# Five raw weight buffers and five ring slots, low parts dealt out by stage, and a bias table made on 128 rows

## The chip, the cores and the metric

One core of a Trainium2 chip runs the whole program. The metric is device time in microseconds, from three runs: 1275.13, 1270.58 and 1267.05, median 1270.58. Engines are named as the profile names them: PE is TensorE, ACT ScalarE, DVE VectorE, POOL GpSimd, SP SyncE.

## The reference

A batch of one, 256 tokens, width 1024, everything in float32. Two hybrid layers come first. Each computes, cut to what matters:

```
p  = split(rmsnorm(x, norm_g) @ w_in)          # 9,312 columns of weights
hm = mlstm(silu(conv4(q, k)), v, gates i, f)   # 4 heads of 256, chunkwise with log gates
hg = gla(q, k, v, log_sigmoid(a @ w_a)/16)     # 4 heads, decay per key channel
hd = top-64 sparse attention(q, k, v, index scores) + rel_bias[t5_bucket(distance)]
x  = x + concat(norms and gates of hm, hg, hd) @ w_out
```

A second block follows: a SwiGLU FFN of width 2816 (added with factor 0.5), a mixer, another such FFN and a last rmsnorm. The mixer takes causal attention with 8 heads and a gMLP branch with spatial products over chunks of 128, multiplies each by its own branch weight and by a sigmoid gate, sums them and multiplies by w_out. Every matrix is used once, for 256 tokens, so the program is a stream of weights.

## The kernel before

Activations lie transposed, channels on partitions and tokens along the free dimension. All weights are cut into 364 slots of 128x1024 float32 (512 KB), numbered in the order of use: 90 slots for each layer (74 in, 16 out), 66 for FFN1, 20 + 16 for the mixer's inputs and gates, 8 branch and 8 output slots, and 66 for FFN2.

Each slot passes a pipeline. SP loads it into one of RAW raw buffers. ACT copies it into one of RING ring slots as fp32r, which keeps the high bits (the high part, L392). Then DVE or POOL subtracts the high part from the raw weight, which gives the low part (L854 as one instruction of 1024 columns, L291 as two halves of 512). PE makes three products per tile, high x high, low x high and high x low, 24 matmuls of 256 columns a slot (L1509 with activations as the moving side, L1557 for the output sums, L1547 with 12 matmuls of 512 columns for value slots). RAW is 3 and RING is 6. The helper `split(p)` makes the part of slot g = p + RING after slot p has been used. ACT waits there for `slots_used` and for the load; DVE takes the low part where g is a multiple of 3, POOL takes the others. The last part releases the raw buffer (semaphores `lo`), and SP then loads slot g + RAW into it.

The order on each engine is written out by hand: every engine walks the slot numbers p, runs the jobs of a table `jobs` (or `jobs2` in the mixer) for that p, and then does its share of `split(p)`. The engines' instruction streams are in order, so a wait in a job holds what stands behind it. The layers are a loop of two iterations over one written-out body; the FFNs are loops over four tiles of three slots (gate, up, down).

At a stage's start the first slots (6 in a layer, 8 in the mixer, 4 in an FFN) run on unnormed activations while the norm factor is computed; `early_result` scales their results. ACT's `norm` and DVE's `norm_lo` (L910) then write the normed activations xs. In slots 16 to 25 of a layer eight levels of the gla decay go round DVE (`level_distance` L1067, `level_queries`, `level_take`), ACT (exponentials), POOL (`level_keys` L318) and PE (L1693). In slots 26 to 41 DVE convolves (L1154).

At the program's very start PE multiplies rel_bias by a one-hot matrix into four rows, ACT copies them to SBUF, and ACT's DMA queue stores them to a DRAM table of [4, 128, 384], each row broadcast 128 times (L438). Skewed reads of that table give the bias tiles later. The index scores reuse the SBUF rows, so they wait until the store is done.

In the mixer `spatial` makes the gMLP product on DVE and writes it to y. For the branch slots ACT and DVE then write the high and low parts of y to ys and xs (`branch_hi` L773, `branch_lo` L1418), and PE waits for four low parts before each half of the first branch slot.

Of the kernel before, what the change touches and what calls it, by code (L numbers as in the profile page):

```python
# [21 lines left out]
F32 = mybir.dt.float32  # L22
# [6 lines left out]
P = 128  # L29
D = 1024  # L30
T = 256
# [3 lines left out]
RAW = 3  # L35
RING = 6
# [8 lines left out]
IN_SLOTS, OUT_SLOTS = 74, 16  # L45
LAYER_SLOTS = IN_SLOTS + OUT_SLOTS
# [42 lines left out]

LEVELS = 8  # L90
# [19 lines left out]
EARLY, M_EARLY = 6, 8  # L110
# [22 lines left out]
def build(nc, d, out):  # L133
    ctx = ExitStack()
    with ctx:
# [63 lines left out]
        bias_row = lg[0:4, 0, 0:HOT]  # L199
        pT = gs  # L200

# [38 lines left out]
        def _(sp):  # L240
            sp.dma_start(raw[:, 0, :], d["w"][0]).then_inc(slot_in[0], 16)
            for c in range(N_UPDATES):
                sp.dma_start(x[:, 2 * c:2 * c + 2, :], d["x"][:, 2 * c:2 * c + 2, :]).then_inc(x_in[c], 16)
            for s in range(1, RAW):
                sp.dma_start(raw[:, s, :], d["w"][s]).then_inc(slot_in[s], 16)
            sp.dma_start(const[:, C_LEV:], d["const"][:, C_LEV:]).then_inc(S["rest_in"], 16)
            sp.dma_start(par2[:], d["par2"]).then_inc(S["par2_in"], 16)
            def load(p, slot, reg=0, per=0):

                sp.wait_ge(lo[p % RAW], reg * (per // RAW) + p // RAW)  # L250
                sp.dma_start(raw[:, p % RAW, :], d["w"][reg * per + slot]).then_inc(slot_in[p % RAW], 16)

            def in_order(first, end):
                n = (end - first) // RAW
                if n:
                    with sp.Fori(0, n) as i:
                        for s in range(RAW):
                            load(first + s, first + s, i, RAW)
                for p in range(first + RAW * n, end):
                    load(p, p)  # L260

            def ffn(at):

                with sp.Fori(0, FFN_TILES - 2) as i:
                    for s, turned in enumerate((1, 2, 0)):
                        load(at + 4 + s, at + 4 + turned, i, 3)

            in_order(RAW, FFN1_AT + 4)
            ffn(FFN1_AT)
            in_order(FFN1_AT + FFN_SLOTS - 2, FFN2_AT + 4)  # L270
            ffn(FFN2_AT)
            in_order(TOTAL_SLOTS - 2, TOTAL_SLOTS)
# [10 lines left out]
        def _(pool):  # L283
            def split(p, reg=0, per=0):

                g = p + RING
                if g % RAW:
# [45 lines left out]
            def ffn(at):  # L333
                for p in range(4):
                    split(at + p)
                loops = (FFN_TILES - 2) // 4 - (1 if at == FFN2_AT else 0)
                with pool.Fori(0, loops) as i:
                    for p in range(12):
                        split(at + 4 + p, i, 12)
                for p in range(at + 4 + 12 * loops, at + FFN_SLOTS):  # L340
                    if p + RING < TOTAL_SLOTS:
                        split(p)
# [21 lines left out]
        def _(act):  # L364
            step = Steps(act, S["act_steps"])
            act.dma_start(par[:], d["par"][0]).then_inc(S["par_in"], 16)
            act.dma_start(rb[:], d["rel"]).then_inc(S["rb_in"], 16)
            act.dma_start(hot, d["hot"]).then_inc(S["rb_in"], 16)
            act.dma_start(const[:, 0:C_LEV], d["const"][:, 0:C_LEV]).then_inc(S["const_in"], 16)
# [46 lines left out]
            def norm(n, g, col, used):  # L416
# [16 lines left out]
            act.wait_ge(S["bias_ps"], 1)  # L433
# [3 lines left out]
            act.wait_ge(S["bias_sb"], 1)  # L437
            act.dma_start(bias_rows.ap(), bias_row.rearrange("h (o n) -> h o n", o=1).broadcast_to((4, P, HOT)))\  # L438
                .then_inc(S["bias_out"], 16)
# [3 lines left out]
            with act.Fori(0, LAYERS) as it:  # L443
# [50 lines left out]
                def gate_softplus():  # L494
                    log_and_exp()
# [21 lines left out]
                def forget_softplus():  # L517
                    log_and_exp()
# [160 lines left out]
            def ffn(at, n, h_done, last):  # L679

                def gate_tanh(f, i=0):
                    act.wait_ge(S["ffn_t"], i * 4 + (h_done + f + 1))
# [3 lines left out]
                def product_hi(f, i=0):  # L686
                    act.wait_ge(S["ffn_h"], i * 4 + (h_done + f + 1))
                    act.activation(ys[:, f % YS, 0, :], ca[:, f % 2, :], ACT.Copy).then_inc(S["y_hi"], 1)  # L688

                def next_split(p, i):  # L690
                    if p + RING < TOTAL_SLOTS:
                        split(p, i, 12)

                def four(i, f0):
                    for f in range(f0, f0 + 4):
                        p = at + 4 + 3 * (f - 2)
                        gate_tanh(f, i)
                        next_split(p, i)
                        product_hi(f, i)
                        next_split(p + 1, i)  # L700
                        next_split(p + 2, i)
# [11 lines left out]
                loops = (FFN_TILES - 2) // 4 - (1 if last else 0)  # L713
                with act.Fori(0, loops) as i:
                    four(i, 2)
                if last:
                    four(0, 2 + 4 * loops)
                else:
# [48 lines left out]
            def branch_hi(k):  # L767
# [5 lines left out]
                act.activation(branch(k, 0), y[:, (k + 4) % 8, :], ACT.Copy).then_inc(S["b_hi"], 1)  # L773
# [1359 lines left out]
```

## Time and profile before

| | before |
|---|---|
| median of three runs | 1270.58 us |
| profiled execution | 1263.89 us, span 1262.0 us |
| mean granted TensorE clock | 0.974 |
| PE busy | 1173.5 us, 93% |
| DVE, ACT, POOL busy | 823.0, 655.4, 698.7 us |
| HBM read | 196.52 MB |

The span runs from the first to the last instruction. A row of a timeline gives start and duration in us, engine, line, operation, output<-inputs with shapes, how many instructions were merged (x24), and in brackets how long the engine had stood idle before it and who released it. Rows by line give the count, the busy time and the mean ns of one, and then the idle time ahead of the group. A row of stretches gives each engine's busy time in it, the granted clock as a share of full speed, the share of DMA time and GB/s. Ends of matmuls are modelled, so two matmul groups are best compared from start to start or for equal counts.

### The profile page before, as it was taken

What the parts mean: (1) busy time and instruction counts of PE and PEld (TensorE: products, weight loads), DVE (VectorE), ACT (ScalarE), POOL (GpSimd) and SP (SyncE); (2) the same over time, 40 slices, a digit from 0 to 9 for tenths busy, and PEclk for the clock granted to TensorE, in tenths of its full rate; (3) what the DMA queues carried; (4) which work ended last, traced back from release to release, by engine and by line L of the source; (5) the groups of instructions that cost most, each with busy time, mean ns of one, the idle gap of its engine ahead of it and who ended that gap; (6) DMA issues with size and microseconds to landing.
All of it is one profiled execution on the core that took longest, in us unless ns stands there. A gap on an engine that the chain in (4) does not pass through costs nothing.

```text
span 1262.0 us, 25299 instructions
## 1 busy us (share of the span) xinstructions
PE 1173.5 (93%) x9214; PEld 1111.7 (88%) x9214; DVE 823.0 (65%) x1301; ACT 655.4 (52%) x1020; POOL 698.7 (55%) x530
## 2 busy tenths in 40 slices
PE   5499998999998989999999999999899889999996
PEld 4488798899997969989999999998878889999996
DVE  4366979486667598866676645555656756655664
ACT  3464485346456637644655544444657435544442
POOL 2243547555655355664566576667565555666662
PEclk9698999999998999999999999999999989999999
DMA  6343334544554433354456455555453445566561
GB/s 208 94 137 122 125 115 150 168 157 163 177 163 149 135 123 105 134 185 143 162 180 204 157 197 189 198 193 185 149 174 127 141 144 175 167 200 200 187 196 50
DMA packets 57715, 199.66 MB, mean 158 GB/s; under 512 B 6388, under 2 KB 9492, under 8 KB 57620
## 3 DMA queue, kind: packets, MB, share of 16 engines
q1 hardware_dynamic: 53856, 193.90, 46.6%
q10 hardware_dynamic: 3764, 4.47, 1.5%
q8 instruction: 62, 1.02, 0.3%
q14 instruction: 33, 0.27, 0.1%
HBM read 196.52 MB, written 1.84 MB: 157 GB/s over the span
## 4 chain that ended last, share of the span: by engine, by line
PE 29%; POOL 28%; issue 23%; DVE 11%; DMA 5%; ACT 3%; POOLq 0%; DVEq 0%; ACTq 0%; SPq 0%
POOL ring L291 26%; PE ps L1509 18%; PE ps L1557 6%; DMA raw<-in_w 5%; PE ps L1547 2%; DVE ring L854 2%; ACT ring L392 1%; DVE gs L1067 1%; PE ps L1660 1%; POOL dec L305 1%; DVE gat L1097 0%; ACT xs L424 0%; DVE xs L1418 0%; DVE xs L864 0%; POOL dec L306 0%
## 5 line engine op out<-in xcount | busy, mean ns | idle before, releaser
L291 POOL TENSOR_TENSOR ring<-raw,ring 128x512 fp32r<-128x512 f32 x484 | 666.8, 1401 | 510.2 <-ACT ring L392 508.8
L1509 PE MATMUL ps<-xs,ring 128*128 128x256 f32 x5424 | 666.7, 283 | 32.9 <-DVE mq L892 15.9
L1509 PEld LDWEIGHTS ps<-xs,ring 128*128 128x128 f32 x5424 | 647.4, 192 | 45.2 <-issue 17.5
L392 ACT ACTIVATE ring<-raw 128x1024 fp32r<-128x1024 f32 x364 | 382.5, 1055 | 251.6 <-DMA raw<-in_w 197.2
L854 DVE TENSOR_TENSOR ring<-raw,ring 128x1024 fp32r<-128x1024 f32 x122 | 179.0, 1467 | 156.6 <-ACT ring L392 154.6
L1557 PE MATMUL ps<-ys,ring 128*128 128x256 f32 x2016 | 240.2, 278 | 4.1 <-DVE ys L916 2.9
L1557 PEld LDWEIGHTS ps<-ys,ring 128*128 128x128 f32 x2016 | 235.8, 188 | 4.8 <-issue 3.5
L1547 PE MATMUL ps<-ring,xs 128*128 128x512 f32 x480 | 120.6, 404 | 6.4 <-DVE xs L910 3.2
L1547 PEld LDWEIGHTS ps<-ring,xs 128*128 128x128 f32 x480 | 88.9, 190 | 28.0 <-issue 9.1
L1154 DVE SCALAR_TENSOR_TENSOR ca<-ps,par,ca 128x253 f32<-128x253 f32 (+2 forms) x96 | 45.1, 477 | 11.4 <-ACT ca L476 10.0
L916 DVE TENSOR_TENSOR ys<-ca,ys 128x256 fp32r<-128x256 f32 x44 | 42.2, 960 | 13.8 <-ACT ys L688 13.8
L683 ACT ACTIVATE ex<-ex 128x256 f32<-128x256 f32 x44 | 18.1, 415 | 61.2 <-DVE ex L1288 61.2
L491 ACT ACTIVATE ex<-ps 128x256 f32<-128x256 f32 x48 | 18.3, 382 | 53.6 <-PE ps L1509 53.5
L916 DVE TENSOR_TENSOR ys<-y,ys 128x256 fp32r<-128x256 f32 x32 | 30.0, 938 | 23.2 <-ACT ys L619 23.1
L1519 PEld LDWEIGHTS ps<-xs,ring 128*128 128x128 f32 x240 | 31.0, 204 | 10.8 <-issue 8.7
L1519 PE MATMUL ps<-xs,ring 128*128 128x256 f32 x240 | 31.9, 297 | 8.8 <-ACT xs L409 5.7
L688 ACT ACTIVATE ys<-ca 128x256 fp32r<-128x256 f32 x44 | 18.2, 413 | 39.4 <-DVE ca L1302 39.3
L1293 DVE SCALAR_TENSOR_TENSOR ca<-ps,rms 128x256 f32<-128x256 f32 x44 | 18.3, 417 | 29.0 <-PE ps L1509 29.0
L1302 DVE SCALAR_TENSOR_TENSOR ca<-ex,ca 128x256 f32<-128x256 f32 x44 | 32.4, 737 | 1.5
L1298 DVE TENSOR_TENSOR ca<-ca,ex 128x256 f32<-128x256 f32 x44 | 30.8, 700 | 1.4
L476 ACT ACTIVATE ca<-ps,par 128x256 f32<-128x256 f32 x32 | 17.8, 557 | 25.4 <-DVE mq L1169 13.8
L538 ACT ACTIVATE gs<-gs 128x256 f32<-128x256 f32 x16 | 6.8, 423 | 45.7 <-DVE gs L1067 45.7
(256 smaller groups left out, 1053.9 us busy)
## 6 DMA issues: line engine op xcount, KB each, us to landing
raw<-in_w SPq DMA_DIRECT2D x364, 512.0 KB, 3.5
y<-bias_rows ACTq DMA_DIRECT2D x6, 256.0 KB, 3.2
x<-in_x SPq DMA_DIRECT2D x4, 256.0 KB, 7.1
out_y<-y SPq DMA_DIRECT2D x4, 256.0 KB, 2.2
const<-in_const SPq DMA_DIRECT2D x1, 896.0 KB, 10.7
bias_rows<-lg ACTq DMA_DIRECT2D x1, 768.0 KB
par<-in_par ACTq DMA_DIRECT2D x3, 181.0 KB, 2.4
dec<-in_wT ACTq DMA_DIRECT2D x1, 512.0 KB, 4.7
```

Of the source, the lines that this page charges most:

```text
L291: last = pool.tensor_tensor(ring[:, g % RING, 1, half], raw[:, g % RAW, half], ring[:, g % RING, 0, half].bitcast(F32), ALU.subtract)
L392: act.activation(ring[:, g % RING, 0, :], raw[:, g % RAW, :], ACT.Copy).then_inc(S["hi"], 1)
L491: ins = act.activation(ex[:, m % 4, :], src[:, 0:T], ACT.Tanh, scale=0.5)
L854: tt(ring[:, g % RING, 1, :], raw[:, g % RAW, :], ring[:, g % RING, 0, :].bitcast(F32), ALU.subtract).then_inc(lo[g % RAW], 1)
L916: tt(ys[:, at, 1, :], src, ys[:, at, 0, :].bitcast(F32), ALU.subtract).then_inc(S["y_lo"], 1)
L1154: ins = stt(dst[:, late:T], bank[:, 0:T - late], w[:, j:j + 1], dst[:, late:T], ALU.mult, ALU.add)
L1298: step(tt(ca[:, f % 2, :], ca[:, f % 2, :], ex[:, 2 + f % 2, :], ALU.mult))
L1302: stt(ca[:, f % 2, :], ex[:, f % 2, :], 1.0, ca[:, f % 2, :], ALU.add, ALU.mult)\
L1509: last = mm(ps[bank][:, half * T:(half + 1) * T], ring[:, slot % RING, wp, (at + k) * P:(at + k + 1) * P], rhs(k, xp), start=(i == 0), sto ...
L1519: return mm(ps[bank][:, 0:T], ring[:, slot % RING, wp, k * P:(k + 1) * P], rhs(k, xp), start=start, stop=stop)
L1547: last = mm(ps[banks[tt]][:, :], xs[:, 2 * q + k, xp, tt * P:(tt + 1) * P], ring[:, slot % RING, wp, k * 512:(k + 1) * 512], start=(q == 0 ...
L1557: ins = mm(ps[4 + n // 2][:, n % 2 * T:(n % 2 + 1) * T], ring[:, slot % RING, wp, n * P:(n + 1) * P], ys[:, at, xp, :], start=(first and n ...
```

## The change

Five things change together.

1. RAW becomes 5 and RING 5, which takes the same SBUF in all. Low parts are dealt out by a function `on_vector(p)`: in the layers' slots 8 to 43 POOL makes all of them, from slot 44 and in the mixer DVE makes every third, and in the FFNs DVE makes those of odd f.
2. The bias table: four matmuls with a broadcast column of rel_bias make 128 equal rows per head, ACT copies four banks, and the store's source has 128 partitions. The small inputs are loaded ahead of the layer parameters, and weight slot 1 ahead of half of x.
3. In a layer's start ACT takes the row results one slot earlier and the gate softplus two slots earlier. The table loads in both softplus jobs are gone.
4. The FFN loops are written out.
5. In the mixer the spatial products move from slots 29 and 31 to 30 and 32, and their result stays in PSUM. The first branch slot waits for each high or low part as it uses it, all high parts first.

```diff
-RAW = 3
-RING = 6
+RAW = 5
+RING = 5
+def on_vector(p):
+    if p < 0:
+        return p in (-RING, -RING + 3)
+    if p < LAYER_SLOTS:
+        if p < EARLY + 2:
+            return p in (3, 6)
+        return p >= 44 and p % 3 == 0
+    if FFN1_AT <= p < MIX_AT or p >= FFN2_AT:
+        f = p - FFN1_AT if p < MIX_AT else p - FFN2_AT
+        return f % 2 == 1 and f < FFN_SLOTS - 4
+    return p % 3 == 0
...
-            sp.dma_start(raw[:, 0, :], d["w"][0]).then_inc(slot_in[0], 16)
-            for c in range(N_UPDATES):
+            fetch(0, 0)
+            for c in range(2):
                 sp.dma_start(x[:, 2 * c:2 * c + 2, :], ...)
+            fetch(1, 1)
+            for c in range(2, N_UPDATES):
+                sp.dma_start(x[:, 2 * c:2 * c + 2, :], ...)
+            for g in range(2, RAW):
+                fetch(g, g)
...
+            for g in range(RAW, TOTAL_SLOTS):
+                sp.wait_ge(lo[g % RAW], g // RAW)
+                fetch(g, stored_at(g))
...
-                if g % RAW:                        # POOL's split
+                if not on_vector(p):
...
-            act.activation(bias_row, ps[5][0:4, 0:HOT], ACT.Copy).then_inc(S["bias_sb"], 1)
+            for h in range(4):
+                act.wait_ge(S["bias_ps"], h + 1)
+                act.activation(relu4[:, h, :], ps[4 + h][:, 0:HOT], ACT.Copy).then_inc(S["bias_sb"], 1)
...
-            act.dma_start(bias_rows.ap(), bias_row.rearrange("h (o n) -> h o n", o=1).broadcast_to((4, P, HOT)))\
+            act.dma_start(bias_rows.ap().rearrange("h p n -> p h n"), relu4).then_inc(S["bias_out"], 16)
...
                 split(1, it, LAYER_SLOTS)
+                row_results()
                 split(2, it, LAYER_SLOTS)
-                row_results()
                 split(3, it, LAYER_SLOTS)
                 norm(it, gains, V_G, it * LAYER_SLOTS + EARLY)
+                gate_softplus()
                 split(4, it, LAYER_SLOTS)
                 split(5, it, LAYER_SLOTS)
-                gate_softplus()
...
-                if g % RAW == 0:                   # DVE's split
+                if on_vector(p):
...
-                loops = (FFN_TILES - 2) // 4 - (1 if last else 0)
-                with dve.Fori(0, loops) as i:
-                    four(i, 2)
+                for f in range(2, FFN_TILES):
+                    tile(f)
...
-                dst = ca[:, pr % 2, :]
+                dst = ps[4 + pr][:, T:2 * T]
-                stt(y[:, pr, :], y[:, pr, :], 0.5, dst, ALU.mult, ALU.mult).then_inc(S["sg_done"], 1)
+                stt(dst, y[:, pr, :], 0.5, dst, ALU.mult, ALU.mult).then_inc(S["sg_done"], 1)
...
-            mm(ps[5][0:4, 0:HOT], rb[:, :], hot, start=True, stop=True).then_inc(S["bias_ps"], 1)
+            for h in range(4):
+                mm(ps[4 + h][:, 0:HOT], rb[:, h:h + 1].broadcast_to((32, P)), hot,
+                   start=True, stop=True).then_inc(S["bias_ps"], 1)
...
-            jobs2[29] = [(spatial, 0), (spatial, 1)]
-            jobs2[31] = [(spatial, 2), (spatial, 3)]
+            jobs2[30] = [(spatial, 0), (spatial, 1)]
+            jobs2[32] = [(spatial, 2), (spatial, 3)]
```

## Rows read from the trace of the kernel before

**Rows 1.** The page: busy time of PE, and DMA issues (size, us to landing).
```profile
PE 1173.5 (93%) x9214; PEld 1111.7 (88%) x9214; DVE 823.0 (65%) x1301; ACT 655.4 (52%) x1020; POOL 698.7 (55%) x530
...
raw<-in_w SPq DMA_DIRECT2D x364, 512.0 KB, 3.5
```

**Rows 2.** Stretches: us, busy by engine, PE clock, DMA share, GB/s.
```profile
22.00:51.00 29.00, 13.05 (x91) 12.75 (x91) 8.12 (x17) 5.14 (x6) 5.88 (x5) 0.71 0.40 90
...
115.00:155.00 40.00, 36.48 (x238) 28.07 (x237) 37.87 (x76) 16.48 (x33) 23.06 (x20) 0.96 0.35 118
...
1019.00:1041.00 22.00, 21.86 (x162) 21.86 (x163) 10.40 (x21) 6.77 (x7) 9.87 (x8) 0.86 0.43 131
```

**Rows 3.** Timeline of PE at the start of layer 1.
```profile
44.31 7.97 PE L1509 MATMUL ps<-xs,ring 128*128 128x256 f32 x48 [15.95 <-DVE mq L892]
...
70.39 0.49 PE L1641 MATMUL ps<-ik,mq 64*128 64x128 f32 x4 [1.66 <-ACTq L457]
```

**Rows 4.** Timeline of ACT at the start of layer 1.
```profile
16.24 1.24 ACTq L438 DMA_DIRECT2D bias_rows<-lg  x1
...
36.25 1.06 ACT L392 ACTIVATE ring<-raw 128x1024 fp32r<-128x1024 f32 x1 [15.93 <-DMA raw<-in_w]
...
53.71 1.06 ACT L392 ACTIVATE ring<-raw 128x1024 fp32r<-128x1024 f32 x1 [10.79 <-DMA raw<-in_w]
```

**Rows 5.** DMA queues, 20 to 60 us: packets, MB, share of 16 engines.
```profile
q10 hardware_dynamic: 482, 0.73, 15.6%
```

**Rows 6.** Timeline of PE at the start of layer 2.
```profile
388.72 11.04 PE L1509 MATMUL ps<-xs,ring 128*128 128x256 f32 x72 [3.71 <-ACT xs L424]
400.98 0.49 PE L1641 MATMUL ps<-ik,mq 64*128 64x128 f32 x4 [1.22 <-ACTq L457]
```

**Rows 7.** Timeline of ACT at the starts of layer 2 and the mixer.
```profile
387.15 1.06 ACT L392 ACTIVATE ring<-raw 128x1024 fp32r<-128x1024 f32 x1 [3.13 <-DMA raw<-in_w]
...
393.03 1.28 ACT L373 ACT_TABLE_LOAD   x1
...
904.46 1.06 ACT L392 ACTIVATE ring<-raw 128x1024 fp32r<-128x1024 f32 x1 [5.39 <-DMA raw<-in_w]
```

**Rows 8.** Groups by line of DVE, 72 to 223 us.
```profile
L854 DVE TENSOR_TENSOR ring<-raw,ring 128x1024 fp32r<-128x1024 f32 x13 | 17.1, 1313 | 4.5 <-ACT ring L392 3.7 <-DVE score L1024 0.5
L1067 DVE TENSOR_TENSOR gs<-gb 128x512 f32<-128x512 f32 x8 | 10.5, 1311 | 1.0 <-PE ps L1693 0.9
```

**Rows 9.** Groups by line of POOL, 155 to 223 us.
```profile
L291 POOL TENSOR_TENSOR ring<-raw,ring 128x512 fp32r<-128x512 f32 x24 | 33.9, 1433 | 29.4 <-ACT ring L392 29.4
```

**Rows 10.** Timeline of PE in FFN1 and in FFN2.
```profile
764.41 5.82 PE L1509 MATMUL ps<-xs,ring 128*128 128x256 f32 x48
...
1153.38 5.60 PE L1509 MATMUL ps<-xs,ring 128*128 128x256 f32 x48
```

**Rows 11.** Timeline of DVE over one tile of FFN2.
```profile
1157.95 0.41 DVE L1288 SCALAR_TENSOR_TENSOR ex<-ps,rms 128x256 f32<-128x256 f32 x1
1159.02 0.42 DVE L1293 SCALAR_TENSOR_TENSOR ca<-ps,rms 128x256 f32<-128x256 f32 x1 [0.66 <-PE ps L1509]
...
1162.85 1.23 DVE L854 TENSOR_TENSOR ring<-raw,ring 128x1024 fp32r<-128x1024 f32 x1 [1.44 <-ACT ring L392]
1163.99 1.51 DVE L916 TENSOR_TENSOR ys<-ca,ys 128x256 fp32r<-128x256 f32 x1
```

**Rows 12.** Timeline of PE in the mixer.
```profile
910.61 2.99 PE L1547 MATMUL ps<-ring,xs 128*128 128x512 f32 x12 [3.22 <-DVE xs L910]
...
993.92 1.44 PE L1933 MATMUL ps<-dec,gv 128*64 128x128 f32 x16 [3.23 <-DVE gv L1405]
...
1019.14 2.93 PE L1509 MATMUL ps<-xs,ring 128*128 128x256 f32 x12 [3.32 <-DVE xs L1418]
```

**Rows 13.** Timeline of DVE in the mixer.
```profile
899.48 1.22 DVE L854 TENSOR_TENSOR ring<-raw,ring 128x1024 fp32r<-128x1024 f32 x1
...
1013.54 5.55 DVE L1418 TENSOR_TENSOR xs<-y,xs 128x256 fp32r<-128x256 f32 x4 [1.80 <-ACT xs L773]
```

More of the change, by code:

```diff
@@ L45 @@
 IN_SLOTS, OUT_SLOTS = 74, 16
+EARLY, M_EARLY = 6, 8
 LAYER_SLOTS = IN_SLOTS + OUT_SLOTS
@@ L109 @@
 N_UPDATES = 4
-EARLY, M_EARLY = 6, 8
 FINAL = LAYERS + 3
@@ L333, in ffn @@
             def ffn(at):
[L334 to L340, printed above, removed]
+                for p in range(at, at + FFN_SLOTS):
                     if p + RING < TOTAL_SLOTS:
@@ L712, in ffn @@
                 split(at + 3)
-                loops = (FFN_TILES - 2) // 4 - (1 if last else 0)
-                with act.Fori(0, loops) as i:
-                    four(i, 2)
-                if last:
-                    four(0, 2 + 4 * loops)
-                else:
+                for f in range(2, FFN_TILES):
+                    tile(f)
+                if not last:
                     act.wait_ge(S["par2_in"], 16)
@@ L1253, in _ @@
                 gate_abs()
-                split(3, it, LAYER_SLOTS)
+                for p in range(EARLY):
+                    split(p, it, LAYER_SLOTS)
                 early_result(4)
@@ L1312, in four @@
-                def four(i, f0):
-                    step.restart()
-                    for f in range(f0, f0 + 4):
-                        p = at + 4 + 3 * (f - 2)
-                        gate(f, p, i)
-                        next_split(p, i)
-                        up(f, p + 1, i)
-                        up_gate(f, i)
-                        product(f, i)
-                        next_split(p + 1, i)
-                        product_lo(f, i)
-                        next_split(p + 2, i)
+                        split(p)
@@ L1325, in ffn, with tile @@
+                def tile(f):
+                    p = at + 4 + 3 * (f - 2)
+                    gate(f, p)
+                    next_split(p)
+                    up(f, p + 1)
+                    up_gate(f)
+                    product(f)
+                    next_split(p + 1)
+                    product_lo(f)
+                    next_split(p + 2)
                 factor(n)
@@ L1334, in ffn @@
                     split(p)
-                loops = (FFN_TILES - 2) // 4 - (1 if last else 0)
-                with dve.Fori(0, loops) as i:
-                    four(i, 2)
-                if last:
-                    four(0, 2 + 4 * loops)
+                for f in range(2, FFN_TILES):
+                    tile(f)
                 update_x(n, at + FFN_SLOTS, 0.25)
@@ L1440, in _ @@
                 normed(LAYERS, c)
-            split(MIX_AT)
-            split(MIX_AT + 3)
+            for p in range(MIX_AT, MIX_AT + 5):
+                split(p)
             for r in range(4, 7):
@@ L1445, in _ @@
             norm_lo(LAYERS, gains2, U_MIX)
-            split(MIX_AT + 6)
+            for p in range(MIX_AT + 5, MIX_AT + M_EARLY):
+                split(p)
             early_result(7)
@@ L1986, in _ @@
                 for g in range(2):
-                    if n == 0:
-                        pe.wait_ge(S["b_lo"], 4 * g + 4)
-                    last = tile_product(n % 4, g, slot, lambda k, part: branch(4 * g + k, part), range(4), at=4 * g)
+                    last = tile_product(n % 4, g, slot, lambda k, part: branch(4 * g + k, part), range(4), at=4 * g,
+                                        ready=(lambda k, part: pe.wait_ge(
+                                            S["b_lo" if part else "b_hi"], 4 * g + k + 1)) if n == 0 else None)
                     if n == KT - 1 and g == 0:
```

140 lines of the change are left out of this document (58 added, 82 removed).

## The prediction

> **What bounds the kernel now.** I read the page first: TensorE (PE) is busy 93% of the span [rows 1], so only what stands between its matmuls can be won. The other engines have room and count only where PE waits for them. The table of stretches says where such places lie [rows 2], PE's timeline names the stall and its releaser [rows 3, 6, 12], and the releasing engine's own timeline says what that engine had waited for [rows 4, 7, 13]. Three kinds of stall come out.
>
> The first is the start. PE stands 15.95 us until 44.31 us, released by the vector engine (DVE) at L892 [rows 3]. DVE only hands on: ScalarE (ACT) stood 15.93 us and then 10.79 us for weight slots [rows 4]. A weight slot normally lands 3.5 us after its issue [rows 1]. Just before, ACT's queue had issued the bias store, 768 KB [rows 4], and from 20 to 60 us that queue's packets hold 15.6% of 16 engines' time [rows 5], while the core moves only 90 GB/s and the granted clock is 0.71 [rows 2]. The second kind is each stage's start (norm and gate scan in layer 2 [rows 6], the mixer [rows 12]). The third is DVE as the late engine: in the level products of a layer it is busy 37.87 of 40 us [rows 2], and it holds PE 3.23 and 3.32 us in the mixer [rows 12]. Inside the FFNs PE doesn't wait, but 48 equal matmuls take 5.82 us in the first FFN and 5.60 in the second [rows 10].
>
> **The change, part by part**, against the profiled execution's 1263.9 us; minus is a gain.
>
> Bias store. Its four heads lay on four partitions, each row broadcast to 128 copies; now PE makes all 128 rows per head, ACT copies four banks, and the store's source has 128 partitions. 15.6% of 16 engines over 40 us is 99.8 engine-us [rows 5]. Evenly on 16 engines it is 6.2 us; packed on the four that match the four source rows it is 25 us, which fits the two waits, 15.93 + 10.79 = 26.7 us [rows 4]. I take 26.7 - 6.2 = 20.5 us won. PE's three more matmuls lie before the first weight is ready, and three more ACT copies (1152 more columns, where 1024 take 1.06 us [rows 4]: 1.2 to 1.5 us) lie ahead of a slot that waits for its DMA anyway. Without the idle the clock stays up: (1 - 0.71) x 29 us is 8.4 us of lost clock [rows 2], most of it in the idle itself; I count 2.5. The second weight goes before half of x, which lets the first products begin about 1 us earlier. The gate softplus moves two high parts up and loses its 1.28 us table load [rows 7]: 2 more. Sum -26; bounds -18 (raw loads still queue behind the store and const) and -30.
>
> The Trainium skill, DMA: Bandwidth & Descriptors, section Why a DMA increments its semaphore by 16 and not by 1, says that the number of engines is the largest up to 16 that divides the slowest dimension of both patterns: 4 before, 16 now. By it the term is the one above; by an even spread before as well it would be near zero.
>
> Start of layer 2. PE waits 3.71 us for ACT's norm, then runs 72 matmuls in 11.04 us where the FFN2 rate gives 8.40, and waits 1.22 us for the row results [rows 6, 10]. ACT's norm stood behind a high part that waited 3.13 us for its DMA [rows 7]; five raw buffers put that load two slots earlier, so this wait goes. The scan chain behind it becomes the next late thing; it starts with a softplus that no longer has a table load and two high parts (about 1.05 us each) ahead. All three together are 7.6 us; I take -5.5, bounds -1 and -7.6.
>
> Slots 8 to 43, twice. DVE loses its low parts: 13 of them, 17.1 us and 4.5 us of waiting ahead of them, between 72 and 223 us [rows 8]. GpSimd (POOL) gets them. From 155 to 223 us it made 24 halves (12 slots) at 1.433 us and waited 29.4 us for ACT [rows 9]; six more slots are 17.2 us, so it still keeps up, with its lead cut from six ring slots to five. The price is contention: L1067, a DVE operation with both inputs in SBUF, runs 1.31 us on average in this stretch, and L916 took 1.51 us beside a running POOL half [rows 8, 11], while PSUM-fed L1293 beside it took 0.42 [rows 11]. Some 60 such two-input operations a layer, up to 0.9 us each for the half that isn't yet delayed, are 27 us against 21.6 us relieved. So DVE's net is from +5 to -15 us a layer. PE can win back at most what it idles: 3.5 us from 115 to 155 us [rows 2], and I allow as much again for the convolution slots after them. I take -2.5 a layer, -5 in all, bounds +10 and -14.
>
> Ends of the layers, first FFN. DVE and POOL take turns by f, and the loops are written out. If the 4% slower rate of the first FFN comes from weights that are just in time, 20 tiles gain 1.5 x 0.22 us each [rows 10], 6.6 us; I allow 1.4 for small stalls at the ends of the stages. I take -8, bounds 0 and -10.
>
> Mixer and branches. Spatial products are asked for one slot (2.7 us) later and waited 3.23 [rows 12]: 2.7 and about 1 of clock. The branch products waited 3.32 us for four low parts in 5.55 us (1.39 each beside POOL) [rows 12, 13]; they now read PSUM, like L1293's 0.42, and PE starts on the high parts: 3.3 gone, with (1 - 0.86) x 22 = 3.1 us of clock [rows 2], of which I count 2. At the start, 3.22 us released by the norm's low parts [rows 12] were DMA lateness again, ACT having waited 5.39 us for weights ahead of the norm [rows 7]: -3; but there a DVE low part that ended at 900.7 us [rows 13] was for the sixth slot ahead and is now for the fifth, needed one slot sooner: +2. Sum -10, bounds -4 and -12.
>
> The second FFN: nothing won or lost; its cover is weighed as rival 3. In all -26 - 5.5 - 5 - 8 - 10 = -54.5: the profiled execution would take 1209.4. It lies 6.7 us below the median of the runs shown (1270.58), so the forecast median is **1216**. The bounds added up straight reach from 73.6 us of gain (1197) to 13 (1258); all bad ends at once are unlikely, so the forecast's own range is 1200 to 1236.
>
> **Rivals.** (1) *Only the start pays.* PE is busy 93% and POOL's lead is shorter; new small waits eat the rest, and the 5.82 us rate comes back by itself. For it: the FFN rates differ without any wait shown. Start -26, mixer -5: 1240. (2) *The store isn't cured*: if its packets are slow because they write rows to HBM, 99.8 engine-us become more on 16 engines and all weight loads crawl together. Then 6 of the 26 are left: 1236. Against it: weight loads of 4 KB rows over all partitions land in 3.5 us [rows 1], and the store's occupied time is a quarter of the engines, as four of 16 would be.
>
> (3) *Slower: the vector chain in the FFNs.* A DVE tile with one low part runs from 1157.95 to 1165.5 us, 7.5 us, 0.66 of it waiting for PE, 1.44 for ACT's high part [rows 11]. Every second tile now has two low parts, both in order between PE-gated steps: 7.5 + 1.23 + up to 1.44 is 10.2, less the 0.66 in both tiles, so 16.4 a pair against PE's 16.8 at most (144 matmuls at 5.60 / 48 [rows 10]; their ends are modelled, so it may be half a microsecond less). It just fits. If POOL stretches the two-input steps further (three steps a tile by 0.9 us, as 1.51 against 0.42 shows), a pair takes up to 21.8: 5.0 x 20 pairs = 100 us, which after the gains is 1316. It decides from 19.5 a pair, where 2.7 x 20 equals the 54.5 won. Against it: the 1.44 us wait overlaps the moved steps, and POOL has a quarter less to do there. A middling case is 1290.
>
> (4) *The port.* GpSimd's work in slots 8 to 43 stretches DVE's two-input operations by the upper bound above, +5 us a layer: +10 in place of -5 is 1231. The Trainium skill, SBUF — State Buffer, section Who interferes with whom, speaks against this part of the change: a DVE instruction with two SBUF inputs and a GpSimd instruction that reads SBUF exclude one another for the whole instruction; by that rule alone every such step waits out a half. The trace agrees (1.51 against 0.42), but PSUM-fed steps, most of DVE's time there, stay free.
>
> **Chances.** Forecast 0.55; only the start 0.18; store not cured 0.07; the vector chain 0.09, of which 0.06 ends slower by over 1%; the port 0.11. A run of this kernel tells no change from 1% (12.7 us), so faster means below 1258. Of the vector chain 0.03, and 0.02 of the store and port cases together with lost small gains, fall within 1%: faster 0.89, same 0.05, slower 0.06. The range, 1198 to 1246, takes in rivals 1, 2 and 4 and leaves out the vector chain and the tails.
>
> **What would show it.** ACT's waits for weights before 60 us shrink from 26.7 us to under 8, and the first index product (70.39 us) [rows 3] comes near 44. Layer 2's stall of 3.71 is gone. ACT's waits for raw weights all but vanish over the whole span. The first FFN's 48 matmuls take 5.60. POOL between 155 and 223 us makes 18 slots without PE waiting for it. Wrong would be: PE idle behind POOL's or DVE's low parts in any stage, FFN tiles over 8.4 us, or DVE busy in slots 18 to 25 as before.

## The result and the profile after

| | before | after |
|---|---|---|
| median | 1269.15 us (4 runs) | 1219.11 us (1213.43 to 1222.02, 4 runs) |
| ratio | 1 | 0.959, 95% interval 0.954 to 0.964 |
| profiled execution | 1263.89 us | 1219.19 us |
| mean granted TensorE clock | 0.974 | 0.984 |

The forecast was 1216 us. A run over 1.5% above the fastest of its kernel (one of e8's and one of b3's below) counts as slow: it is in the medians and ranges given, but not in the ratios. To see where the 44.7 us of the two profiled executions went, I cut PE's timeline at points that every version has: the first index product of a layer, and the first product of each stage. The last stage ends at the last sum of squares. Lengths in us; in brackets what matmul spacing adds, explained below.

| stage | before | after | difference | forecast |
|---|---|---|---|---|
| start to index product | 70.39 | 42.79 | -27.6 | -26 |
| body of layer 1 | 296.94 [1.7] | 296.88 [0.6] | -0.1 | about -2.5 |
| start of layer 2 | 33.65 | 28.62 | -5.0 | -5.5 |
| body of layer 2 | 289.82 [0.6] | 293.87 [2.3] | +4.1 | about -2.5 |
| FFN1 | 192.66 [5.5] | 188.56 [6.9] | -4.1 | -8, with layer ends |
| mixer and branches | 183.75 [2.5] | 171.32 [1.9] | -12.4 | -10 |
| FFN2 | 181.38 [0.2] | 182.00 [0.2] | +0.6 | 0 |

The page after: busy time of PE, and the DMA issues that answer to [rows 1].
```profile
PE 1169.0 (96%) x9220; PEld 1106.9 (91%) x9220; DVE 833.0 (68%) x1294; ACT 643.7 (53%) x1019; POOL 735.9 (60%) x544
...
raw<-in_w SPq DMA_DIRECT2D x364, 512.0 KB, 3.7
...
bias_rows<-lg ACTq DMA_DIRECT2D x1, 768.0 KB, 5.9
```
PE does the same work in a shorter span; DVE is busier than before (823.0), although it makes fewer low parts (115 against 122). The store now lands 5.9 us after its issue.

Stretches of the kernel after that answer to [rows 2], same columns: the start, the level products, the branches.
```profile
14.00:42.00 28.00, 26.43 (x213) 25.72 (x212) 23.42 (x39) 19.69 (x34) 18.45 (x14) 1.00 0.68 230
87.00:127.00 40.00, 35.10 (x235) 27.36 (x234) 38.45 (x69) 15.48 (x28) 30.80 (x26) 0.96 0.37 112
988.00:1010.00 22.00, 20.76 (x180) 20.59 (x179) 15.97 (x25) 10.02 (x15) 12.15 (x10) 1.00 0.60 191
```
The start moves 230 GB/s (14 to 42 us) where it moved 90 (22 to 51 us), with the clock at 1.00 instead of 0.71. In the level products DVE is busy 38.45 of 40 us, as before, and PE less than before.

PE's timeline after, at the starts of layer 1 and 2, FFN1's tiles, and the mixer (answers to [rows 3, 6, 10, 12]).
```profile
22.05 19.41 PE L1506 MATMUL ps<-xs,ring 128*128 128x256 f32 x168
42.79 0.49 PE L1640 MATMUL ps<-ik,mq 64*128 64x128 f32 x4 [1.33 <-ACTq L463]
...
172.19 16.16 PE L1506 MATMUL ps<-xs,ring 128*128 128x256 f32 x120 [4.00 <-DVE ca L1155]
...
339.67 7.42 PE L1516 MATMUL ps<-xs,ring 128*128 128x256 f32 x48 [2.43 <-ACT xs L415]
...
368.29 0.49 PE L1640 MATMUL ps<-ik,mq 64*128 64x128 f32 x4 [1.28 <-ACTq L463]
...
683.87 5.89 PE L1506 MATMUL ps<-xs,ring 128*128 128x256 f32 x48 [0.38 <-POOL ring L303]
...
692.43 5.82 PE L1506 MATMUL ps<-xs,ring 128*128 128x256 f32 x48
...
867.94 8.42 PE L1506 MATMUL ps<-xs,ring 128*128 128x256 f32 x72 [1.61 <-DVE ring L855]
...
960.09 1.14 PE L1923 MATMUL ps<-dec,gv 128*64 128x128 f32 x16 [1.42 <-DVE gv L1401]
...
1092.51 5.60 PE L1506 MATMUL ps<-xs,ring 128*128 128x256 f32 x48
```
The stalls of 15.95 and 3.71 us are gone: 168 matmuls run in one piece where PE stood. At the convolutions each layer has one stall of 4.00 us, where before had two (1.95 and 1.40 in layer 1, 1.95 and 1.80 in layer 2). FFN1 still takes 5.82 us for 48 matmuls and FFN2 5.60. In all traces 256-column matmuls follow one another at 113.35 or at 117.8 ns, at the same granted clock of 1.00, for stretches of up to 175 us; the brackets of the table are the matmuls at the longer spacing times 4.4 ns. An FFN of 1580 such matmuls is 6.9 us longer at it.

Groups by line after, in layer 1 from 44.4 to 195.4 us (count, busy us, mean ns, idle ahead); they answer to [rows 8, 9].
```profile
L1068 DVE TENSOR_TENSOR gs<-gb 128x512 f32<-128x512 f32 x8 | 12.7, 1582 | 1.0 <-PE ps L1692 0.9
...
L1143 DVE SCALAR_TENSOR_TENSOR y<-y,gains,rms 128x256 f32<-128x256 f32 x4 | 3.8, 1006 | 0.0
...
L303 POOL TENSOR_TENSOR ring<-raw,ring 128x512 fp32r<-128x512 f32 x69 | 94.6, 1398 | 37.3 <-ACT ring L398 36.7
```
L1068 is before's L1067, which took 1311 ns.

### The profile page after: what moved, and what is told of

Same layout as the page of the kernel before. It is cut to its first block, busy times and chain, and to the rows that moved or that the text cites. A ratio compares the mean times of both kernels' runs of the same rounds, so it can differ in the third digit from the quotient of the medians.

```text
span 1217.3 us, 23627 instructions
## 1 busy us (share of the span) xinstructions
PE 1169.0 (96%) x9220; PEld 1106.9 (91%) x9220; DVE 833.0 (68%) x1294; ACT 643.7 (53%) x1019; POOL 735.9 (60%) x544
## 4 chain that ended last, share of the span: by engine, by line
PE 76%; DVE 16%; ACT 3%; issue 3%; POOL 1%; DMA 1%; ACTq 0%; DVEq 0%
PE ps L1506 43%; PE ps L1554 17%; PE ps L1544 6%; DVE gs L1068 2%; DVE ring L855 1%; PE ps L1783 1%; ACT ring L398 1%; PE ps L1659 1%; DVE xs L865 1%; POOL ring L303 1%; DVE xs L911 1%; PE ps L1692 1%; DVE gat L1098 1%; DVE y L1143 1%; PE ps L1516 1%
## 5 line engine op out<-in xcount | busy, mean ns | idle before, releaser
L303 POOL TENSOR_TENSOR ring<-raw,ring 128x512 fp32r<-128x512 f32 x498 | 705.8, 1443 | 443.2 <-ACT ring L398 441.4
L1506 PE MATMUL ps<-xs,ring 128*128 128x256 f32 x5424 | 657.3, 281 | 10.3 <-DVE ca L1155 8.0
L1506 PEld LDWEIGHTS ps<-xs,ring 128*128 128x128 f32 x5424 | 638.9, 190 | 21.7 <-issue 11.1
L398 ACT ACTIVATE ring<-raw 128x1024 fp32r<-128x1024 f32 x364 | 377.7, 1051 | 109.4 <-PE ps L1554 45.0
L855 DVE TENSOR_TENSOR ring<-raw,ring 128x1024 fp32r<-128x1024 f32 x115 | 163.6, 1423 | 123.4 <-ACT ring L398 123.0
L917 DVE TENSOR_TENSOR ys<-y,ys 128x256 fp32r<-128x256 f32 x32 | 32.9, 1037 | 12.8 <-ACT ys L623 12.8
L1294 DVE SCALAR_TENSOR_TENSOR ca<-ps,rms 128x256 f32<-128x256 f32 x44 | 18.5, 420 | 29.5 <-PE ps L1506 29.5
L1516 PEld LDWEIGHTS ps<-xs,ring 128*128 128x128 f32 x240 | 32.2, 211 | 4.2 <-ACT xs L415 2.6
L1516 PE MATMUL ps<-xs,ring 128*128 128x256 f32 x240 | 33.0, 302 | 2.7 <-ACT xs L415 2.4
L1692 PEld LDWEIGHTS ps<-qke 64*128 64x128 f32 x240 | 14.9, 187 | 15.4 <-issue 15.1
```

The lines of the kernel that those rows point to most:

```text
L303: last = pool.tensor_tensor(ring[:, g % RING, 1, half], raw[:, g % RAW, half], ring[:, g % RING, 0, half].bitcast(F32), ALU.subtract)
L398: act.activation(ring[:, g % RING, 0, :], raw[:, g % RAW, :], ACT.Copy).then_inc(S["hi"], 1)
L855: tt(ring[:, g % RING, 1, :], raw[:, g % RAW, :], ring[:, g % RING, 0, :].bitcast(F32), ALU.subtract).then_inc(lo[g % RAW], 1)
L917: tt(ys[:, at, 1, :], src, ys[:, at, 0, :].bitcast(F32), ALU.subtract).then_inc(S["y_lo"], 1)
L1506: last = mm(ps[bank][:, half * T:(half + 1) * T], ring[:, slot % RING, wp, (at + k) * P:(at + k + 1) * P], rhs(k, xp), start=(i == 0), sto ...
L1516: return mm(ps[bank][:, 0:T], ring[:, slot % RING, wp, k * P:(k + 1) * P], rhs(k, xp), start=start, stop=stop)
```

## Experiments

Each version is judged by its median and by the same cuts of its own trace, one profiled execution each. The versions ran in four batches: e1 to e4, e5 to e8, b0 to b2, and b3. The kernel before, run again beside each, had a median of 1270.34, 1263.89, 1272.21 and 1268.07 us; the changed kernel ran again only in b0. So medians of different batches compare only to some 8 us, and the ratios are each to before in the same batch (0.959 for the changed kernel). The bodies of the layers scatter too: layer 2's is 289.8 us in before and 295.1 in e1 with the same layer code, and 293.8 to 299.0 in after, b0, e2, e7 and e8.

**The store alone, in the kernel before (e1), and the old store in the changed kernel (e2).**
```diff
...
-bias_row = lg[0:4, 0, 0:HOT]                 # e1 on before; e2 the reverse on after
+relu4 = lg[...].rearrange("p (h n) -> p h n", h=4)
...
-act.dma_start(bias_rows.ap(), bias_row...broadcast_to((4, P, HOT)))
+act.dma_start(bias_rows.ap().rearrange("h p n -> p h n"), relu4)
...
```


> The kernel before with the bias table made on 128 rows and nothing else; raw buffers stay 3. Theory (the start's gain is the store's source rows, 4 partitions against 128): ACT's waits of 15.93 and 10.79 us are gone, the store lands in 5 to 8 us, and about 20 to 24 us of the 27.6 us of the start come back: 1245 to 1249 us. Rival (five raw buffers and the earlier second weight give most of the start): under 10 us won, 1260 or more.


Measured: 1248.24 us, ratio 0.984 (0.979 to 0.990). The index product comes at 51.47 us, 18.9 earlier, a little under the 20 to 24 of the theory. The store lands in 4.8 us, and ACT's longest wait for a weight behind it is 4.28 us in place of 15.93, as its timeline in e1 shows:
```profile
37.63 1.06 ACT L392 ACTIVATE ring<-raw 128x1024 fp32r<-128x1024 f32 x1 [4.28 <-DMA raw<-in_w]
```


> The changed kernel with the old store (four source partitions, each row broadcast 128 times). Theory: five raw buffers and two more loads in flight don't hide a store that holds the queue's engines; ACT waits over 15 us for weights again and the time is 18 to 24 us over the changed kernel's 1219: 1237 to 1243. Rival (deeper buffers would have hidden it): under 1228.


Measured: 1235.0 us, ratio 0.973 (0.969 to 0.977); index product at 51.87 us, 9.1 later than after. ACT's timeline:
```profile
36.58 1.06 ACT L398 ACTIVATE ring<-raw 128x1024 fp32r<-128x1024 f32 x1 [7.34 <-DMA raw<-in_w]
39.13 1.06 ACT L398 ACTIVATE ring<-raw 128x1024 fp32r<-128x1024 f32 x1 [1.50 <-DMA raw<-in_w]
```
So the two cures overlap. The store alone wins 18.9 us. The rest of the change without it wins 18.5, and both together win 27.6. I put the overlap down to the five buffers, which would ride out most of a slow store. That is argued: no run has the old store with three buffers and all else new. My expectation for e2 was too high: the waits are 8.8 us, not 15, and the time is 2 us under the range.

**Slots 8 to 43 shared again (e3), and the low parts that moved there left out (e5).**
```diff
-        return p >= 44 and p % 3 == 0              # e3
+        return p % 3 == 0
-                        half = slice(a, a + SLOT // 2)   # e5, POOL's split
+                        left_out = p < LAYER_SLOTS and EARLY + 2 <= p < 44 and p % 3 == 0
+                        half = slice(a, a + (8 if left_out else SLOT // 2))
```


> The changed kernel with the vector engine making every third low part in slots 8 to 43 again, as before. Theory (relief eaten by contention: about 13 low parts a layer leave DVE, but POOL's extra halves stretch DVE's other two-input steps by as much): no change, 1215 to 1223, DVE's busy share in slots 18 to 25 as it is. Rival A (the relief is worth something, and something else in the body took it): slower by 5 to 15 us. Rival B (giving all to POOL costs more than it brings): faster by 3 to 8 us, and the wait of 4.00 us at the convolution slots falls to 2 or less.


Measured: 1225.71 us (1214.64 to 1229.08); its ratio's interval, 0.957 to 0.971, overlaps that of after (its median is 3 us above the theory's range). Its profiled execution happens to have the long spacing in both FFNs, 20.6 us of it in all against 12.1. Without spacing the last cut is at 1191.1 us, against 1191.9. No difference: theory. Where each wait goes is not the same, as PE's waits show, first e3, then after (total us, times, longest).
```profile
PE ps L1692 <- DVE gat L1096: 4.6, 2, 2.3
PE ps L1544 <- DVE ca L1155: 4.3, 2, 2.3
PE ps L1506 <- DVE ca L1155: 3.9, 2, 2.0
...
PE ps L1692 <- DVE gat L1098: 0.8, 3, 0.4
```
```profile
PE ps L1506 <- DVE ca L1155: 8.0, 2, 4.0
...
PE ps L1692 <- DVE gat L1096: 5.7, 2, 2.9
PE ps L1692 <- DVE gat L1098: 4.0, 6, 1.0
```
With the low parts back on DVE, PE waits *less* for the level products (5.4 us against 9.7) and the same at the convolutions (8.2 against 8.0). DVE's own steps say why; these are e3's groups by line over the stretch shown above for after:
```profile
L1068 DVE TENSOR_TENSOR gs<-gb 128x512 f32<-128x512 f32 x8 | 9.3, 1159 | 2.4 <-PE ps L1692 2.3
...
L1143 DVE SCALAR_TENSOR_TENSOR y<-y,gains,rms 128x256 f32<-128x256 f32 x4 | 1.8, 497 | 0.0
```
With POOL's extra halves they take 1582 and 1006 ns, in both layers. Without them they take 1159 and 497 here, 1308 and 496 in e3's layer 2, and 1311 and 496 in before, although DVE makes every third low part in these.

> The changed kernel, with the low parts that POOL took over in slots 8 to 43 (every third) cut to 8 columns of each half, so that neither engine makes them; the low parts of those slots are left out of the products. DVE is as free as the change makes it, and POOL's extra halves are gone. Theory (contention ate the relief): the level waits fall from 2.93 + 0.57 + 0.43 + 0.97 us to under 3 in all, the 4.00 us at the convolutions to under 2.5, DVE's two-input steps get shorter (L1068 from 1.58 us to 1.4 or less), and the layers' bodies lose 3 to 6 us each with the clock they cost: 1209 to 1215. Rival (DVE's own chain, the gla norm in one piece, sets these waits whoever makes the low parts): both waits stay within 1 us of what they are, 1217 to 1221.


Measured: 1216.68 us (1214.41 to 1221.25). The median misses the 1209 to 1215 of the theory and is no clear gain (ratio 0.963, 0.960 to 0.966), but the profiled run has the long spacing in both FFNs (21.3 us in all). The bodies of the layers, where the edit lies, are 290.7 and 290.0 us against 296.9 and 293.9, and without spacing 288.6 and 287.4 against 296.3 and 291.6: 7.7 and 4.2 us shorter. Of layer 1's 7.7 some 3 are clock (granted 0.98 against 0.97), which scatters between profiles of one program. Groups by line, layer 1, same stretch as above (L1069 is L1068 of after):
```profile
L1069 DVE TENSOR_TENSOR gs<-gb 128x512 f32<-128x512 f32 x8 | 9.1, 1138 | 3.7 <-PE ps L1693 3.6
...
L1144 DVE SCALAR_TENSOR_TENSOR y<-y,gains,rms 128x256 f32<-128x256 f32 x4 | 1.8, 495 | 0.0
```
The only thing taken from after is POOL's work, and DVE's L1068 falls from 1582 to 1138 ns, the norm's rows from 1006 to 495. PE's waits at the levels are 2.06 us a layer, at the convolutions 1.94, together 4.0 in place of 8.9. This holds in both layers. So the relief was real and POOL's halves took it back. The rival, DVE's own chain, holds only for what is left.

**Buffers back to 3 and 6 (e4).**
```diff
-RAW = 5
-RING = 5
+RAW = 3
+RING = 6
```


> The changed kernel with 3 raw buffers and 6 ring slots; the dealing of low parts stays. Theory: the buffers are worth the stalls behind late loads at the stages' starts only (layer 2 about 3 us, mixer about 3 us, first weights 1 us): 1224 to 1229, and the first FFN's 48 matmuls stay where they are at 5.82 or wherever this program has them, because late weights are not what slows them. Rival (buffers also carry the first FFN's gain of 4 us and more of the body): 1232 or more. Rival two (six ring slots are worth as much as five raw buffers): 1219 to 1221.


Measured: 1228.34 us, ratio 0.968 (0.964 to 0.973). The start is 4.9 us longer, the mixer 1.1 and FFN1 (without spacing) 1.4. The start of layer 2 is 29.56 us, without spacing 28.9 against 28.5, although ACT waits for a weight there. The bodies are 1.1 and 3.9 us longer, the second within what layer 2's body scatters, and FFN2 is 1.0 longer. I had expected 3 us for layer 2, 3 for the mixer and 1 for the first weights: the total came out (1224 to 1229), its parts did not. ACT at the start of layer 2:
```profile
358.74 1.06 ACT L398 ACTIVATE ring<-raw 128x1024 fp32r<-128x1024 f32 x1 [2.64 <-DMA raw<-in_w]
```
ACT's waits for raw weights are 170.6 us over the span here and 13.4 after, so 157 us more of ACT's waiting went with 9 us more time: that sum is no measure of PE's.

**ACT's old order at a layer's start (e6).**
```diff
                 split(1, it, LAYER_SLOTS)
-                row_results()
                 split(2, it, LAYER_SLOTS)
+                row_results()
...
-                gate_softplus()
                 split(4, it, LAYER_SLOTS)
                 split(5, it, LAYER_SLOTS)
+                gate_softplus()                # with its table load, as forget_softplus
```


> The changed kernel with ACT's old order at a layer's start: row results one slot later, gate softplus after two more high parts, and the table loads in both softplus jobs. Run e4 had the start of layer 2 at 29.6 us with three raw buffers, so buffers are not what shortened it from 33.6. Theory: the order is; the start of layer 2 goes back to 31 to 33 us and the program's start loses 2 to 4 us: 1224 to 1227. Rival (DVE's low parts moved behind the norm's do it): the start of layer 2 stays under 30 and the time under 1222.


Measured: 1236.45 us, ratio 0.977 (0.975 to 0.979). The time is 9 us above the range of the theory. Start +3.0 us, start of layer 2 30.79 (+2.2), bodies +5.4 and +3.0 (the second within the scatter); of the medians' 17 us some 10 are in the profile without spacing, and the rest is not explained. By the medians this set of small moves is worth about as much as the store's shape in e2 (16 us). The start of layer 2 does not go back to 33.6, so neither the buffers nor this order alone brings its 5.0 us back. Either they cover for one another, as the cures of the start do, or DVE's low parts do it, which now stand behind the norm's; I tested neither the two together nor those low parts.

**Branches through SBUF (e7).**
```diff
-                dst = ps[4 + pr][:, T:2 * T]
+                dst = ca[:, pr % 2, :]
-                stt(dst, y[:, pr, :], 0.5, dst, ...)
+                stt(y[:, pr, :], y[:, pr, :], 0.5, dst, ...)
+                    if n == 0:
+                        pe.wait_ge(S["b_lo"], 4 * g + 4)
```


> The changed kernel with the spatial result written to y again and the first branch slot waiting for four low parts per half; the spatial products stay in slots 30 and 32. Theory: the 3.3 us wait for low parts comes back, with 2 to 3 us of clock behind it: mixer and branches 176 to 178 us against 171.3, 1224 to 1227. Rival (with the spatial products one slot later and five buffers the low parts are in time anyway): within 1 us of 171.3.


Measured: 1231.49 us (1225.23 to 1233.09). Mixer and branches 175.91 us against 171.32. DVE's low parts of the branches, in e7 and then in after:
```profile
969.80 5.56 DVE L1414 TENSOR_TENSOR xs<-y,xs 128x256 fp32r<-128x256 f32 x4 [1.80 <-ACT xs L774]
```
```profile
975.39 1.42 DVE L1414 TENSOR_TENSOR xs<-ps,xs 128x256 fp32r<-128x256 f32 x4 [1.77 <-ACT xs L774]
```
The same four subtractions take 5.56 us with both inputs in SBUF and 1.42 with one in PSUM, and PE's wait of 3.33 us returns; POOL's halves ran beside both. The median is 12 us over after's and over 4 above the range of the theory, where the profiled run, the fastest of five, shows 6; the rest is not explained. Its FFN1, the same code as after's, ran at the short spacing: 182.48 us.

**FFN low parts by threes (e8).**
```diff
-        return f % 2 == 1 and f < FFN_SLOTS - 4
+        return f % 3 == 0
```


> The changed kernel with DVE making every third low part in the FFNs, to the last slot, as before; the loops stay written out. Theory (the first FFN's gain of 4 us came from the stalls at its start and end, 1.13 behind a low part and 2.99 before the mixer, and the matmul spacing of 113 or 118 ns falls as it does in any run): about 3 to 4 us of waits come back at the first FFN's ends, none inside, 1220 to 1225. Rival (the dealing sets the spacing): all tiles of the first FFN fall to 8.2 us or rise to 8.5 together with those of the second.


Measured: 1226.35 us (1219.45 to 1243.19). Each FFN gets one wait, of 2.52 and 2.71 us, near its start, and none at its end or inside. The theory had 3 to 4 us at FFN1's ends and 1220 to 1225. The spacing is short in both FFNs, as the rival said for the first; but e7, with the new dealing, has it short in FFN1 too, so the dealing alone does not set it. The stall of 2.99 us that before had between FFN1 and the mixer is in before and, as 1.72, in e1, the two with looped FFNs; it is missing in e8 (old dealing) and e4 (old buffers). The written-out loops are the likeliest of the things that those two share with after and not with e1, but no run tests them alone. PE's timeline of the kernel before, at that place:
```profile
883.46 2.71 PE L1519 MATMUL ps<-xs,ring 128*128 128x256 f32 x21 [2.99 <-ACT xs L409]
```

**Versions that build on this.** b1 is the changed kernel with four edits (its label says five):
```diff
-            with pe.Fori(0, LAYERS) as it:
+            for it in range(LAYERS):
...
-                product_hi(0)
-                product_hi(1)
                 split(at + 2)                      # ACT, an FFN's start
+                product_hi(0)
+                product_hi(1)
...
-    return p % 3 == 0
+    return p % 3 == 0 and p != MIX_AT
-                        30: [(gla_mean,)], 32: [(gla_norm,)],
+                        30: [(gla_mean,)], 32: [(gla_norm,)], 34: [(gla_scale, 0)], 35: [(gla_scale, 1)],
+                        36: [(gla_scale, 2)], 37: [(gla_scale, 3)],
```


> The changed kernel with four small edits at the waits that its trace still shows: gla_norm keeps its refinement in slot 32 and scales its four rows in slots 34 to 37 one by one; PE's loop over the two layers is written out; in an FFN ACT makes the high part after slot 2 ahead of the two products; the mixer's first low part goes from DVE to POOL. Theory (these waits are orders, not loads): the 4.00 us at the convolutions fall under 1 in both layers with most of the clock behind them (2 to 5 us a layer), the 2.4 to 3 us before layer 2 shrink to under 1, the 0.38 us behind POOL in the FFNs and the 1.61 us in the mixer go: 1199 to 1208 against 1219. Rival (the chain is as long as it was and only moves): waits turn up at slots 34 to 40 instead, 1214 to 1220.

> The four edits, and DVE makes every third low part in slots 8 to 43 again. Theory (who makes them is a draw, as e3 said): within 2 us of the kernel with the four edits alone, level waits 2.3 us in place of 4.9, convolution waits a little longer. Rival (with the norm out of the way DVE has room, and POOL's contention is what is left): 3 to 6 us faster than it.

> The changed kernel itself, unedited, run again beside the two others for a direct comparison: 1213 to 1222 us. Its stages are the same to 0.5 us where they have the same matmul spacing; each FFN is 182 us at a spacing of 113 ns or 188.5 at 118, and which it is may differ from the first profile (first FFN 188.6, second 182.0). If spacing belonged to the program, both would be as they were.


Measured on one chip: b0 1218.71 us (1214.88 to 1227.66), b1 1220.33 (1212.91 to 1225.61), b2 1210.34 (1207.25 to 1213.94). b1: the rival in substance, and far from the theory's 1199 to 1208. With PE's loop written out the stall before layer 2 is gone, and the mixer's 1.61 us too. But the 4.00 us at the convolutions became 1.08, 0.67 and 3.41, more in sum, and the FFNs' 0.38 became 1.48 and 1.27, because POOL's half now ran beside DVE's chain. DVE in b2's FFN1 and then at the same place in b0:
```profile
669.36 1.11 DVE L1302 TENSOR_TENSOR ca<-ca,ex 128x256 f32<-128x256 f32 x1
670.51 1.40 DVE L1306 SCALAR_TENSOR_TENSOR ca<-ex,ca 128x256 f32<-128x256 f32 x1
```
```profile
678.59 0.42 DVE L1299 TENSOR_TENSOR ca<-ca,ex 128x256 f32<-128x256 f32 x1
679.04 0.42 DVE L1303 SCALAR_TENSOR_TENSOR ca<-ex,ca 128x256 f32<-128x256 f32 x1
```
b2 is faster than both, by 8 to 10 us: the rival again, and more than it said. Its waits are 2.7 us at the levels and 3.9 at the convolutions, a layer. b0's cuts repeat after's, but for layer 2's body (297.0 us against 293.9), with the same spacing in both FFNs. By b0's own sign that speaks for a spacing that belongs to the program; e5 and e6, whose FFN2 is the same code in a program that differs elsewhere, had the long one there.

The last version moves the norm out of the crowded stage, and makes one low part of the FFN earlier:
```diff
-32: [(gla_norm,)], 34: [(gla_scale, 0)], 35: ..., 36: ..., 37: [(gla_scale, 3)],   # from b2
...
+42: [(gla_norm,)], 44: [(ml_weight, 0), (gla_scale, 0), (gla_scale, 1)],
+45: [(ml_weight, 1), (gla_scale, 2), (gla_scale, 3)],
...
                     gate(f, at + 2 * f)
+                    if f:
+                        split(at + 1)
                     up(f, at + 2 * f + 1)
```


> b2 with two more moves on DVE: the whole gla_norm goes behind the convolutions (refinement in slot 42, its four rows in slots 44 and 45), where DVE stood idle 4.72 and 3.50 us in the changed kernel; and in an FFN's start DVE makes its first low part (for slot 6) in the idle 1.6 us ahead of the second up product. Theory (a lump of 9 us in a stage where DVE has no room is what holds PE at the convolutions): the waits of 0.71, 0.96 and 2.24 us a layer fall under 1 in all and no new one over 1 turns up at slots 42 to 46; the 1.08 and 1.27 us in the FFNs go; 1200 to 1206 against 1210. Rival (the convolutions' own two-input steps beside POOL hold PE): over 2 us of waits stay between slots 26 and 41, 1208 to 1212. Rival two (the norm now delays the mlstm weights): a wait of 2 us or more behind L1175 or its like at slots 44 to 46.


Measured: **1200.24 us** (1192.63 to 1210.70), ratio 0.945 (0.940 to 0.951) against 0.960 (0.955 to 0.965) for b0. Bodies of the layers 289.96 and 287.53 us, FFN1 181.67, FFN2 181.41. PE's waits in b3, those of the layers:
```profile
PE ps L1697 <- DVE gat L1096: 4.6, 2, 2.3
...
PE ps L1697 <- DVE gat L1098: 0.8, 3, 0.4
PE ps L1769 <- DVE pml L1177: 0.7, 2, 0.4
```
No wait at the convolutions is left, and the norm costs about 0.35 us a layer where it now stands. The theory held; the two moves were made together, so what each is worth in time is read from the stages, not from runs.

## Why the prediction was right, and where it was not

The sum was -54.5 us. The median fell by 50.0 and the profiled execution by 44.7; the 5 us between them are that before's profiled execution lies 5.3 us under its median. Two terms missed by 13 us together, and two gave 4 more than forecast. The forecast had added 6.7 us to its sum for such a gap, but the changed kernel has none (1219.19 profiled, 1219.11 the median). So the sum missed by 9.8 us (1209.4), the forecast of 1216 by 3, and that it came so near is in part luck. Of my signs of being wrong three showed up: PE idle behind low parts (1.61 us in the mixer, 0.38 in the FFNs), tiles of FFN1 at 8.48 us, and DVE as busy in the level products as before.

*Start*, -26 against -27.6. Right in size and cause: ACT's waits for the store are gone, the index product is at 42.79, and the clock holds. The queue's packets, 10 to 40 us after, against [rows 5]:
```profile
q10 hardware_dynamic: 528, 0.79, 7.0%
```
That is 33.6 engine-us (7.0% of 16 engines over 30 us) for as many bytes as took 99.8; I had spread the same 99.8 over more engines, so the store was cheaper still. What I did not see is that the parts are not additive (e1, e2). I booked 20.5 us to the store's shape and nothing to the buffers; the store's shape alone is worth 18.9 of the 27.6, the rest of the change without it 18.5, and in the changed kernel going back costs 9.1 for the shape, 4.9 for the buffers (e4) and 3.0 for the order (e6).

*Start of layer 2*, -5.5 against -5.0. The size is right, but the cause I gave is not borne out, so the size is luck. The step said that five raw buffers take the 3.13 us wait for a weight away and with it the 3.71 us stall. In e4 ACT still waits 2.64 us and PE doesn't stand. Going back costs 2.2 us for the order (e6) and about 0.4 for the buffers (e4); where the rest of the 5.0 comes from stays open.

*Slots 8 to 43*, -5 against +4.0. The failed step is the relief: "DVE's net is from +5 to -15 us a layer", of which I took a gain. e3 shows the move to be worth nothing, and e5 with e3 why: leaving the low parts out altogether shortens a body by some 4 to 8 us whether it is set against after (POOL makes them) or against e3 (DVE makes them), so POOL's halves cost what the relief brings. I had named this as rival 4 and priced it upwards only from the bound. The +4.1 of layer 2 is not shown to be a cost of the change: its clock loss, (1 - granted clock) times length, is 2.9 us before, and 5.9 and 8.9 in two profiles of the same changed program (297.0 us in the second), and e1, whose layers are before's, takes 295.1 us there.

*Ends and FFN1*, -8 against -4.1. The failed step is "if the 4% slower rate of the first FFN comes from weights that are just in time". It does not: ACT's waits for raw weights fell from 197.2 to 13.4 us and the rate stayed, while e4, with 170.6 us of such waits, has most of its first FFN at the shorter spacing; the rate is 5.60 in e7 and e8, and 5.82 in FFN2 too in e5. What was won are stalls that I had put at 1.4 us: without spacing 187.2 us became 181.7, 2.99 of it at the hand-over to the mixer. Why the first FFN ran at the slower rate stays open.

*Mixer*, -10 against -12.4. e7 gives 4.6 us for the branches (5.4 without spacing) where I had 5.3; spatial's wait fell by 1.8 us (3.23 to 1.42), not 2.7; the fifth slot's low part costs 1.61, where I had +2. The norm's wait is gone, and e4, with 2.44 us behind DVE's norm, says that this one was the buffers. The clock gave 5.5 us back in place of the 3 I booked.

*FFN2*, 0 against +0.6. The slower rival stayed away: PE waits for no tile, each takes 8.16 us, and a pair, 16.3, had to reach 19.5.

## What to carry to other kernels

When work moves from the vector engine to GpSimd, price it at what GpSimd does to the steps that stay, and look whether those have two SBUF inputs; a step that can read one input from PSUM stays out of it (5.56 us against 1.42). A long wait of a feeding engine for its loads says nothing until the bound engine stands behind it. A lump of 9 us on an engine without room belongs in a stage where it idles (b3), not cut up where it is (b1).

## What the runs showed of the hardware

- DVE and POOL. The same step of 256 columns took 0.42 us alone and 1.11 to 1.40 beside a running POOL half. The Trainium skill, SBUF — State Buffer, section Who interferes with whom, says that a DVE instruction with two SBUF inputs contends with a GpSimd instruction that reads SBUF, over a shared pair of ports that is an exclusive lock. 5.56 us against 1.42 for four subtractions, with POOL running beside both, agrees.
- Two spacings of matmuls, 113.35 and 117.8 ns, at a granted clock of 1.00. Some stretches begin or end at waits, but in before FFN1 turns from short to long near 741 us, and PE waits for nothing there. Profiles of the same FFN code have either (an FFN is 6.9 us longer), while the one program profiled twice, after and b0, has the same in both FFNs. So it is not shown that it varies between runs of one program, or that it makes their scatter; it can have hidden e5's gain in its median. What chooses it stays open.
- PE stood 1.8 to 3.75 us at the turn of its loop over the layers in before and in every version with the loop, in some with no releaser but "issue" (3.75 in e2, 3.05 in e6); with the loop written out (b1 to b3) PE goes on at once.
